# First-layer attention scores as split fp32r products, with compressed weights, column sums and half tiles at later places

## What is computed

```python
kc = compress(k_cmp, ...)                       # 31 compressed keys
s_c = einsum(q, kc) * scale - slope * dist_c    # masked
p_c = softmax(s_c) * valid_c                    # compressed weights
s_s = einsum(qc, ksg) * scale - slope * dist_s  # selected keys, causal
s_w = einsum(qc, kw) * scale - slope * dist_w   # window keys, causal
o = g0 * (p_c @ vc) + g1 * (softmax(s_s) @ v_sel) + g2 * (softmax(s_w) @ v_win)
...
mod = silu(c) @ ada_w + ada_b                   # six vectors for the second block
h = rms_norm(x) * (1 + scale_m) + shift_m
proj = h @ w_in_2 + b_in_2
```

## Time and profile before

| | us |
|---|---|
| median of 3 runs | 1374.02 (1372.23 to 1377.24) |
| profiled execution | 1372.39 |
| its span, first to last instruction | 1370.7 |
| TensorE busy | 1357.2 |
| VectorE busy | 802.8 |
| GpSimd busy | 601.6 |
| ScalarE busy | 598.4 |

### The profile page before, as it was taken

How to read it: one execution, slowest core, us unless ns; L and a number is a source line. 1 busy time by engine, 2 the same in 40 slices (tenths; PEclk the granted TensorE clock), 3 DMA queues, 4 the chain that set the end, 5 groups by cost and what they waited for, 6 DMA issues and landing times.

```text
span 1370.7 us, 20826 instructions
## 1 busy us (share of the span) xinstructions
PE 1357.2 (99%) x7562; PEld 1132.7 (83%) x7562; DVE 802.8 (59%) x1622; ACT 598.4 (44%) x1030; POOL 601.6 (44%) x322
## 2 busy tenths in 40 slices
PE   8999999999999999999999999999999999999998
PEld 7877777778998888888888978888998888888887
DVE  5897965456778676767896869533562323231222
ACT  7223545464264445453223435575364434442222
POOL 7532222216354444445544479533354444444441
PEclk9999999999999999999999999999999999999999
DMA  7931111015525444445663231021223322223221
GB/s 219 225 93 62 32 62 47 17 47 168 171 86 176 141 155 148 149 126 170 195 214 99 76 93 62 32 63 31 93 93 107 107 92 92 92 88 103 93 85 62
DMA packets 188309, 146.14 MB, mean 107 GB/s; under 512 B 21561, under 2 KB 186659, under 8 KB 188240
## 3 DMA queue, kind: packets, MB, share of 16 engines
q1 hardware_dynamic: 186528, 144.59, 34.4%
q10 hardware_dynamic: 1200, 0.36, 0.1%
q0 software_dynamic: 512, 0.25, 0.1%
HBM read 143.08 MB, written 2.10 MB: 106 GB/s over the span
## 4 chain that ended last, share of the span: by engine, by line
PE 90%; DVE 7%; DMA 2%; issue 1%; ACT 0%; DVEq 0%; SPq 0%; ACTq 0%
PE ps L2148 26%; PE ps L2149 26%; PE ps L2150 26%; DVE ps L1752 3%; PE ps L2584 2%; PE ps L2335 2%; PE ps L2390 1%; DMA ada<-in_ada_w 1%; PE ps L2419 1%; PE ps L2655 1%; PE ps L2611 1%; PE ps L2640 1%; DMA x_in<-in_x 0%; PE ps L2677 0%; DVE ps L1757 0%
## 5 line engine op out<-in xcount | busy, mean ns | idle before, releaser
L789 POOL TENSOR_TENSOR w_lo<-raw,w_hi 128x1024 fp32r<-128x1024 f32 (+2 forms) x224 | 516.1, 2308 | 698.6 <-ACT w_hi L856 433.8
L2148 PE MATMUL ps<-h_hi,w_hi 128*128 128x512 f32 (+1 forms) x1336 | 502.5, 376 | 0.6 <-DVE h_lo L1387 0.6
L2149 PE MATMUL ps<-h_lo,w_hi 128*128 128x512 f32 (+1 forms) x1336 | 493.8, 370 | 0.0
L2150 PE MATMUL ps<-h_hi,w_lo 128*128 128x512 f32 (+1 forms) x1336 | 493.7, 370 | 0.0
L2148 PEld LDWEIGHTS ps<-h_hi,w_hi 128*128 128x128 f32 x1336 | 252.1, 189 | 61.5 <-issue 17.9
L2150 PEld LDWEIGHTS ps<-h_hi,w_lo 128*128 128x128 f32 x1336 | 252.2, 189 | 43.2
L2149 PEld LDWEIGHTS ps<-h_lo,w_hi 128*128 128x128 f32 x1336 | 252.4, 189 | 40.7 <-issue 0.5
L856 ACT ACTIVATE w_hi<-raw 128x1024 fp32r<-128x1024 f32 (+2 forms) x136 | 133.4, 983 | 228.7 <-PE ps L2150 207.9
L1126 ACT ACTIVATE w_hi<-raw 128x1024 fp32r<-128x1024 f32 x88 | 93.2, 1059 | 212.3 <-PE ps L2150 212.3
L2148 PE MATMUL ps<-g_hi,w_hi 128*128 128x512 f32 (+1 forms) x394 | 144.9, 368 | 0.0
L2149 PE MATMUL ps<-g_lo,w_hi 128*128 128x512 f32 (+1 forms) x394 | 144.4, 366 | 0.0
(11 more groups left out here) (365 smaller groups left out, 1686.0 us busy)
## 6 DMA issues: line engine op xcount, KB each, us to landing
ada<-in_ada_w SPq DMA_DIRECT2D x48, 512.0 KB, 3.9
raw<-in_ffn_w_up SPq DMA_DIRECT2D x22, 1024.0 KB, 4.9
raw<-in_w_up SPq DMA_DIRECT2D x22, 1024.0 KB, 4.9
raw<-in_w_in SPq DMA_DIRECT2D x21, 1024.0 KB, 5.1
raw<-in_ffn_w_down SPq DMA_DIRECT2D x8, 896.0 KB, 5.7
raw<-in_w_down SPq DMA_DIRECT2D x8, 896.0 KB, 4.6
raw<-in_w_in SPq DMA_DIRECT2D x16, 256.0 KB, 3.7
raw<-in_w_out SPq DMA_DIRECT2D x4, 1024.0 KB, 5.2
```

What stands on the lines that cost most here:

```text
L789: pool.tensor_tensor(w_lo[slot % 4][:, 0:nk, :], part[:, :, slot % 2 * P:(slot % 2 + 1) * P], w_hi[slot % 4][:, 0:nk, :].bitcast(F32), ALU ...
L2148: pe.matmul(out_ap, w, x, start=first, stop=False, **kw)
L2149: pe.matmul(out_ap, w, xl, start=False, stop=False, **kw)
L2150: return pe.matmul(out_ap, wl, x, start=False, stop=last, **kw)
```

## The change

1. The first attention's scores become fp32r products. The keys of a branch and group are held as 128 rows: high part in the group's own 64 rows, low part in the other 64. The queries are held twice, high part in both halves, and low part in both halves. Two products of 128 rows replace one fp32 product of 64, and steps of 128 columns are made 256 wide. ScalarE makes the high parts and doubles the low ones (`keys_high`, `keys_doubled`, `queries_high`, `queries_doubled`), GpSimd subtracts (`keys_low`, `queries_low`). Keys are staged in `acc`, the copies lie in buffers that are free at the time.
2. The compressed scores of the last two pairs of heads are still added to their bias at step 0, but their minimum and subtraction come at step 9, their exponentials at step 10 and their weights at steps 12 and 14. The weights are made for two pairs at a time.
3. A running sum of the layer norm moves from `rstd` to `qT[:, 2, :]`.
4. `ada_sums` comes behind part 19 instead of 18.
5. The first halves of tiles S_FH and S_FH+1 are made in turn, as their second halves were.

```diff
@@ constants
+        HIGH_KEYS = {(0, 0): KD + 1, (0, 1): KD + 2, (1, 0): KD + 3, (1, 1): KD + 8}
+        HIGH_QUERIES = [KD + 3, KD + 8, KD + 12, KD + 16]
+        LOW_KEYS = {(0, 0): 1, (0, 1): 2, (1, 0): 3, (1, 1): 6}
+        LOW_QUERIES = [3, 6, 8, 10]
+        LOW_BEHIND = {S_K + 4: 2, S_K + 5: 3, S_MERGE: 5, S_MERGE + 1: 8, S_MERGE + 2: 10, S_MERGE + 10: 12}
+        KEYS_READY = [HEADS + 2, HEADS + 6]
+        QUERIES_READY = [HEADS + 5, HEADS + 8, HEADS + 10, HEADS + 12]
...
@@ gpsimd
+            def keys_low(b, g):
+
+                pool.wait_ge(high_parts, HIGH_KEYS[b, g])
+                pool.wait_ge(low_or_gated, LOW_KEYS[b, g] - 1)
+                pool.tensor_tensor(staged_keys(b)[OWN[g], :], staged_keys(b)[OWN[g], :], keys[b][g][OWN[g], :].bitcast(F32),
+                                   ALU.subtract).then_inc(low_or_gated, 1)
+
+            def queries_low(i):
+
+                for g in range(2):
+                    pool.wait_ge(high_parts, HIGH_QUERIES[i] + 2 * g + 1)
+                    pool.wait_ge(low_or_gated, LOW_QUERIES[i] + g)
+                    pool.tensor_tensor(queries[i][g][1][OWN[g], :], qT[OWN[g], i, :],
+                                       queries[i][g][0][OWN[g], :].bitcast(F32), ALU.subtract).then_inc(low_or_gated, 1)
...
+                if s in LOW_BEHIND:
+                    pool.wait_ge(lo_done, s + 1)
+                if s == S_K + 4:
+                    keys_low(0, 0)
+                    keys_low(0, 1)
+                if s == S_K + 5:
+                    keys_low(1, 0)
+                if s == S_MERGE:
+                    queries_low(0)
+                if s == S_MERGE + 1:
+                    keys_low(1, 1)
+                    queries_low(1)
+                if s == S_MERGE + 2:
+                    queries_low(2)
+                if s == S_MERGE + 10:
+                    queries_low(3)
+                if s in LOW_BEHIND:
+                    pool.wait_ge(low_or_gated, LOW_BEHIND[s])
...
@@ scalar
+            def queries_high(i):
+
+                for g in range(2):
+                    for rows_to in (OWN[g], OTHER[g]):
+                        act.activation(queries[i][g][0][rows_to, :], qT[OWN[g], i, :], ACT.Copy).then_inc(high_parts, 1)
+
+            def queries_doubled(i):
+
+                for g in range(2):
+                    act.wait_ge(low_or_gated, LOW_QUERIES[i] + (2 if i == PAIRS - 1 else g + 1))
+                    act.activation(queries[i][g][1][OTHER[g], :], queries[i][g][1][OWN[g], :].bitcast(F32),
+                                   ACT.Copy).then_inc(bias_and_queries, 1)
...
                 evac(s, qT[:, s - S_Q, :], scale=-SCALE)
+                i = s - S_Q
+                if i == 2:
+                    keys_doubled(1, 1)
+                if i:
+                    queries_doubled(i - 1) if i < 3 else None
+                if i == 1:
+                    act.wait_ge(cmp_kv_done, 1)
+                    keys_high(1, 1)
+                if i < 3:
+                    if i == 0:
+                        act.wait_ge(hid_done, 1)
+                    act.wait_ge(freed["act"], FREED[s][1])
+                    queries_high(i)
...
+                if j == 7:
+                    queries_doubled(2)
+                if j == 10:
+                    compressed_exponentials(1)
+                if j == 12:
+                    act.wait_ge(cx_ready, 4)
+                    queries_high(3)
+                if j == 14:
+                    queries_doubled(3)
...
@@ vector
+                        if pair and m + 1 == IN_PSUM[1]:
+                            dve.wait_ge(bias_and_queries, KEYS_READY[1])
...
             scaled_weights(0)
-            compressed_scores(1)
+            for g in range(2):
+                compressed_added(g, 1).then_inc(cx_ready, 1)
             for j in range(1, NI + 1):
                 if j < NI:
                     row_minimum(j)
-                if j < 5:
-                    compressed_weights((j - 1) // 2, (j - 1) % 2)
+                if j < 3:
+                    compressed_weights(j - 1, 0)
+                if j == 9:
+                    dve.wait_ge(cx_ready, 4)
+                    for g in range(2):
+                        compressed_lowered(g, 1)
+                if j in (12, 14):
+                    compressed_weights((j - 12) // 2, 1)
...
@@ tensor
-                L = (t + 1) * P
+                L = max(t + 1, 2) * P
+                if (t, b) == (0, 0):
+                    pe.wait_ge(bias_and_queries, QUERIES_READY[i])
+                if t == 0 and i == 0:
+                    pe.wait_ge(bias_and_queries, KEYS_READY[b])
                 for g in range(2):
-                    grp = slice(g * DH, (g + 1) * DH)
                     if j:
                         pe.wait_ge(scores_ready, 2 * j + g - 1)
-                    pe.matmul(ps[4 + g][:, 0:L], qT[grp, i, t * P:(t + 1) * P], kT[grp, b, 0:L],
-                              start=True, stop=True).then_inc(qk_done, 1)
+                    for part in range(2):
+                        ins = pe.matmul(ps[4 + g][:, 0:L], queries[i][g][part][:, t * P:(t + 1) * P], keys[b][g][:, 0:L],
+                                        start=part == 0, stop=part == 1)
+                    ins.then_inc(qk_done, 1)
...
-                if n == 18:
+                if n == 19:
                     ada_sums()
...
             for half in range(2):
-                for j in range(4):
-                    if (half, j) == (1, 0):
-                        second_halves(S_FH, h_hi, h_lo, lambda k: pe.wait_ge(half_lo, PIECES + KD + k + 1))
-                    if half and j < 2:
-                        continue
+                two_halves(S_FH, half, h_hi, h_lo, lambda k: pe.wait_ge(half_lo, PIECES + KD * half + k + 1))
+                if half == 0:
+                    column_sums(1)
+                for j in range(2, 4):
```

More of the change, by code:

```diff
@@ L256, in build @@
         cv_hi = sb("cv_hi", [P, CC, T], F32R, at=z_at)
+        keys = [[sb("keys_00", [P, T], F32R, at=k_at), sb("keys_01", [P, T], F32R, at=k_at + 4 * T)],
+                [sb("keys_10", [P, T], F32R, at=rstd_at), sb("keys_11", [P, T], F32R, at=w2_at)]]
+        queries_at = [[mg_at + 4 * T * (3 + 4 * i + n) for n in range(4)] for i in range(PAIRS - 1)]
+        queries_at.append([mg_at + 4 * T * (2 * KD - 1), cbias_at, cbias_at + 4 * T, G0 + 4 * T * (PAIRS - 1)])
+        queries = [[[sb(f"queries_{i}{g}{part}", [P, T], F32R, at=queries_at[i][g if i == PAIRS - 1 and part == 0 else
+                                                                               2 + g if i == PAIRS - 1 else 2 * g + part])
+                     for part in range(2)] for g in range(2)] for i in range(PAIRS)]
         kv_at = G0 + 4 * PAIRS * T
@@ L1592, in _, with compressed_low @@
             dve.tensor_scalar(vcN[0:NCMP, :], ps[7][0:NCMP, 64:64 + P], 0.5, None, ALU.mult).then_inc(cmp_kv_copied, 1)
[L1593 to L1599, removed]
-                    link(dve.tensor_tensor(x, by_head(ps[6 + g][:, :].rearrange("p (n m) -> p n m", m=32)),
-                                           by_head(cbias[:, g * 16:(g + 1) * 16, :]), ALU.add))
-                    low = stat[:, 32 + 16 * g:48 + 16 * g].rearrange("p (t i) -> p t i", i=PAIRS)[:, :, half]
-                    link(dve.tensor_reduce(low, x, AX.X, ALU.min))
-                    dve.tensor_tensor(x, x, low.unsqueeze(3).to_broadcast([P, QT, 2, NCMP]),
-                                      ALU.subtract).then_inc(cx_ready, 1)
+            def compressed_low(g, pairs):
+                low = stat[:, 32 + 16 * g:48 + 16 * g].rearrange("p (t i) -> p t i", i=PAIRS)
+                return low[:, :, 2 * pairs:2 * pairs + 2]
@@ new lines, in compressed_added, with compressed_lowered @@
+            def compressed_added(g, pairs):
+                by_head = lambda v: v.rearrange("p (t i) m -> p t i m", i=PAIRS)[:, :, 2 * pairs:2 * pairs + 2, 0:NCMP]
+                dve.wait_ge(cqk_done, 2 * pairs + g + 1)
+                return dve.tensor_tensor(cp_part(g, pairs), by_head(ps[6 + g][:, :].rearrange("p (n m) -> p n m", m=32)),
+                                         by_head(cbias[:, g * 16:(g + 1) * 16, :]), ALU.add)
+            def compressed_lowered(g, pairs):
+                x, low = cp_part(g, pairs), compressed_low(g, pairs)
+                link(dve.tensor_reduce(low, x, AX.X, ALU.min))
+                dve.tensor_tensor(x, x, low.unsqueeze(3).to_broadcast([P, QT, 2, NCMP]),
+                                  ALU.subtract).then_inc(cx_ready, 1)
```

119 lines of the change are left out of this document (74 added, 45 removed).

## The result

| | before | after |
|---|---|---|
| median, us | 1374.24 (1372.23 to 1377.24) | 1358.34 (1357.97 to 1362.77) |
| profiled execution | 1372.39 | 1357.97 |
| TensorE busy | 1357.2 | 1347.2 |

The ratio is 0.9883 (0.986 to 0.9906): 1.2% faster, 15.9 us between the medians and 14.4 between the profiled executions. The direction and the mechanism of the work were as forecast. The size was not: I gave 1362.3, and my range ended at 1358.7, 0.4 us above the result.

What follows compares the result with a forecast made beforehand. TensorE, busy 99% of the span, was taken as the bound. Gains of 6.3 + 0.9 + 3.2 + 1.3 = 11.7 us took 1372.39 to 1360.7; 1.63 added for the median gave 1362.3, range 1358.7 to 1368.5.

Steps and rivals of the forecast that it cites:

- Scores, 6.3 us: First attention, 32 score steps: four fp32r products of 128 rows replace the fp32 ones, 6.3 us less, bounds 1.8 and 7.
- the step behind transposes: 16 of 32 score steps follow transposes: gain 0.35 us each, 0.14 at 128 columns, 5.0 us in all.
- Behind values: The other 16 score steps, behind weighted values: gain 0.15 us each, loss 0.06 at 128 columns, 1.35 us in all.
- C: Rival: narrow fp32r products are held by weight loads, so the scores bring only 1.8 us: 1366.8 us; chance 0.07.
- D: Rival: no new score product's weight load is hidden, 128 products cost 0.189 us more each: 1386 us; chance 0.02.
- Stall at step 3, 0.9: First attention: moving compressed-weight work lets VectorE scale before GpSimd's subtraction, ending TensorE's wait for `sc`: 0.9 us, bounds 0 and 0.9.
- E: Rival: ScalarE becomes the pace, all 17.6 us of its added copies lie on the path: 1380 us; chance 0.03.
- What is added beside TensorE, nothing: New work on ScalarE (17.6 us), GpSimd (14 us) and VectorE (1.6 us at step 12) is covered and costs nothing.
- Rival B: New GpSimd subtractions or ScalarE copies collide; TensorE waits at steps 9 to 15, 2 to 6 us: 1364 to 1368; chance 0.16.
- Later sums, 3.2: Down projection: another tile ahead of `ada_sums` fills TensorE's idle time there: 3.2 us, bounds 2 to 3.2.
- Half tiles, 1.3: Behind the second norm: half tiles in turn fill waits for `h_lo` pieces: 1.3 us, bounds 0 and 1.66.
- one thing: TensorE's 1.2 GHz clock from 941.8 to 945.2, behind one-column products, may fall away or recur: 1.5 us either way.

Runs made afterwards that it cites:

- both doublings: Changed kernel with ScalarE's sixteen copies of the high queries made twice: 1366.98 us with six GpSimd subtractions also doubled, 1367.03 us without.
- the third series: The changed kernel, unedited, measured again on the chip of other follow-up runs: 1358.91 us (before 1374.7), ratio 0.9887.
- the second's: The changed kernel, unedited, measured again beside other follow-up runs on one chip: 1360.35 us (before 1374.2), ratio 0.9899.
- the first series: The original measurement of the whole change against the kernel before: 1358.34 us (before 1374.24), ratio 0.9883.

## Why the prediction was wrong, point by point

- **What bounds the kernel: right.** All of the work won is won on TensorE.
- **Scores, 6.3 us: 6.75.** The mechanism and the step behind transposes were right to 0.02 us: 0.35 against 0.35, 0.33 and 0.33 (256, 384, 512 columns), 0.14 against 0.14 (128). Behind values, 0.15 was forecast and 0.158, 0.148 and 0.131 measured, and -0.054 against -0.06 at 128. What I mis-sized is the count: steps 14 and 16 stand behind the fp32 products of the layer norm, and the first behind other work. Step 14 gains 0.34 and step 0 0.14, where I had booked 0.15 and -0.06; step 1 gains less than booked. Rivals C and D fell with the 0.56 us of four products. (Two slips of the working change nothing: 128 x 0.09 is 11.5, not 11.7, and D and E together had 0.05, not 0.04.)
- **Stall at step 3, 0.9: 1.1 with what the starts regain.** The cause, VectorE held for the length of GpSimd's subtraction, and the cure are shown by the run that moved the weights back. Its worth there is 2.2 us; my bound of 0.9 took TensorE as it was.
- **What is added beside TensorE, nothing: right in the result, and the margin mis-stated.** A copy of 64x512 costs 0.65 us between starts, not 0.55 (the row's 1.15 us for two already say 0.57), a subtraction of 64x512 on GpSimd 1.3, not 1.2, and at the tanh some 0.6 us are left instead of a tile. Rival B was nearer than its 0.16: 2.65 us more on ScalarE there made it true, as both doublings show.
- **Later sums, 3.2: 3.15. Half tiles, 1.3: 1.25**, both within their bounds. The next late at the halves was what I had named.
- **The clock: the step that failed.** I added 1.63 us to come from the profiled execution to the median, as if it were a constant, and took the low stretch as "one thing" worth 1.5 us that could come or go at one place. The runs showed an offset of 1.63 us before and 0.37 after. The likeliest reading is that the 1.63 was itself a second low stretch of the typical execution, behind the idle time ahead of `ada_sums`; the profiled one happened to have none there. The change removes that idle time, and the offset goes with it. For it speaks the run with the idle time filled, 1.9 us with no work removed; the run with the idle time put back cost no more than the idle time and doesn't bear it out. The sum of the work, 11.7, was right to 1.1 us (12.8). From 1362.3 to 1358.34 it is 1.1 us of work, 1.6 for the stretch at 942 that the profiled execution had and this series didn't, and 1.3 for the offset (1.63 forecast, 0.37 measured).
- **The range.** Its lower end allowed for one stretch less and 1 us of scatter, but kept the 1.63 on top. With the offset taken as a stretch it would have reached to 1357.1. With the third series' 1358.91 or the second's 1360.35 the forecast range holds, so that the first series fell outside is in part the luck of three executions in four without a stretch; the error of the middle, 1.9 to 4.0 us, stays in each.

What stays open: what decides in an execution whether the stretch comes. The same kernel on the same chip shows both.

## What to carry to other kernels

A difference between a profiled execution and the median of the same kernel need not be a constant that can be added: look at the mean clock of each execution, and ask whether the change takes away what brings the difference about. An idle time of 3 us on an otherwise full TensorE can cost more than its length: in three of five traces here the clock fell at it or behind it, which cost 1.25 to 2.5 us more. A stall's length in the trace can be less than what its cure is worth, once other edits make the waiting engine earlier; and the cover of work "beside" the bound is measured best by doubling it.

## What the hardware showed that was not expected

- Without any change in the work, filling a 3 us idle time of TensorE raised the mean granted clock from 0.997 to 0.999 or 0.998 in ten of eleven executions and took 1.9 us from the median. Put back into the changed kernel, the idle time cost its own 3.1 us and no more.
- Products of 128 columns in fp32r start 0.11 us apart, those of 256 at 0.12: under 256 the columns no longer set the pace, and the 0.188 us weight loads don't either.
- In these rows the extra cost of a change between kinds of products falls on whichever fp32r product comes first: the tile's second product follows its first after 0.34 us in the earlier trace rows and after 0.23 when scores of its own kind stand before it.
- VectorE and GpSimd again: a scaling of 1.00 us took 3.12 and 3.21 us in the two traces shown, where GpSimd's subtraction of 1024 columns started within 0.1 us of it. This agrees with the Trainium skill, SBUF — State Buffer, "Who interferes with whom".
